# First five products begin on half of the features, and eight early transfers get a buffer each

## What is computed

```
mod = silu(c) @ w_ada + b_ada                     # 6 x 1024 columns
sh1, sc1, g1, sh2, sc2, g2 = split(mod, 6)
h   = rms_norm(x, norm1_w) * (1 + sc1) + sh1
p   = h @ w_in                                    # q, k, v, z, a, beta, ...
q, k, v = silu(causal_conv4(p[q, k, v]));  q, k = l2_normalize(q), l2_normalize(k)
g    = -exp(a_log) * softplus(p[a] + dt_bias);  beta = sigmoid(p[beta])
o    = gated_delta_rule(q, k, v, g, beta)         # 8 heads, chunks of 64
```

## Time and profile before

| | us |
|---|---|
| median of 3 runs | 970.33 (969.82 to 974.45) |
| profiled execution, its own time | 974.01 |
| its span, first to last instruction | 972.2 |
| PE busy in it | 926.5 |
| DVE busy | 667.2 |
| ACT busy | 504.9 |

### The profile page before, as it was taken

The page is one execution under the profiler, slowest core; times in us unless marked ns, Lnnn a source line. Parts: engine busy times, 40 slices in busy tenths (PEclk is TensorE's granted clock), DMA queues, the critical chain, the costliest instruction groups (busy, mean ns, idle before and its releaser), DMA issues.

```text
span 972.2 us, 18558 instructions
## 1 busy us (share of the span) xinstructions
PE 926.5 (95%) x7996; PEld 880.7 (91%) x7996; DVE 667.2 (69%) x1113; ACT 504.9 (52%) x821; POOL 65.2 (7%) x91
## 2 busy tenths in 40 slices
PE   5789999999999999999989999989999999999997
PEld 2588888898899999989989999979998999999997
DVE  3876677557579986778758875465656677777643
ACT  2476666544344556455334444465565566665442
POOL 0100012011000000030000001010000300000001
PEclk9799999999999999999999999999999999999999
DMA  8743222232249985446898775515343345555631
GB/s 321 265 157 127 88 88 91 85 131 88 88 158 359 351 299 219 174 179 253 253 290 318 265 241 186 197 43 197 131 140 108 107 177 196 186 174 166 235 120 44
DMA packets 27681, 177.31 MB, mean 182 GB/s; under 512 B 2864, under 2 KB 5680, under 8 KB 7504
## 3 DMA queue, kind: packets, MB, share of 16 engines
q1 hardware_dynamic: 27600, 176.13, 51.5%
HBM read 174.29 MB, written 1.84 MB: 181 GB/s over the span
## 4 chain that ended last, share of the span: by engine, by line
PE 71%; DVE 12%; ACT 7%; DMA 7%; issue 2%; SPq 0%; DVEq 0%; ACTq 0%
PE ps L1002 38%; PE ps L1008 19%; DVE wl L1696 3%; DMA raw<-in_w_fi_dram 3%; DVE acc L1631 2%; ACT wh L1343 2%; PE ps L1000 2%; DMA raw<-in_ada_dram 1%; DMA raw<-in_w_rest_dram 1%; DVE tmp L1658 1%; PE ps L1046 1%; DMA raw<-in_w_sc_dram 1%; PE ps L1140 1%; PE ps L1054 1%; PE ps L1201 1%
## 5 line engine op out<-in xcount | busy, mean ns | idle before, releaser
L1002 PE MATMUL ps<-HH,wh 128*128 128x256 f32 x1480 | 388.0, 294 | 6.4 <-DVE wl L1696 5.5
L1696 DVE TENSOR_TENSOR wl<-raw,wh 128x1024 fp32r<-128x1024 f32 x265 | 321.4, 1233 | 97.2 <-ACT wh L1343 96.5
L1002 PE MATMUL ps<-HH,wl 128*128 128x256 f32 x1480 | 375.2, 285 | 0.0
L1343 ACT ACTIVATE wh<-raw 128x1024 fp32r<-128x1024 f32 x265 | 272.6, 1040 | 171.8 <-PE ps L1008 105.3
L1002 PEld LDWEIGHTS ps<-HH,wh 128*128 128x128 f32 x1480 | 287.1, 194 | 15.8 <-issue 8.0
L1002 PEld LDWEIGHTS ps<-HH,wl 128*128 128x128 f32 x1480 | 287.1, 194 | 2.1 <-issue 2.1
L1008 PE MATMUL ps<-HL,wh 128*128 128x256 f32 x1480 | 241.5, 286 | 2.6 <-DVE HL L1671 2.2
L1008 PEld LDWEIGHTS ps<-HL,wh 128*128 128x128 f32 x1480 | 207.3, 194 | 3.3 <-DVE HL L1671 2.6
L1002 PE MATMUL ps<-FH,wl 128*128 128x256 f32 x352 | 88.8, 285 | 0.0
L1002 PE MATMUL ps<-FH,wh 128*128 128x256 f32 x352 | 88.1, 279 | 0.0
L1631 DVE SCALAR_TENSOR_TENSOR acc<-raw,silc,acc 128x512 f32<-128x512 f32 x101 | 76.6, 758 | 8.4 <-DMA raw<-in_ada_dram 5.2
(11 more groups left out here) (251 smaller groups left out, 1090.1 us busy)
## 6 DMA issues: line engine op xcount, KB each, us to landing
raw<-in_ada_dram SPq DMA_DIRECT2D x32, 1024.0 KB, 5.3
raw<-in_w_fi_dram SPq DMA_DIRECT2D x22, 1024.0 KB, 4.9
raw<-in_w_up_dram SPq DMA_DIRECT2D x22, 1024.0 KB, 4.8
raw<-in_w_rest_dram SPq DMA_DIRECT2D x20, 1024.0 KB, 4.8
raw<-in_w_in_dram SPq DMA_DIRECT2D x16, 1024.0 KB, 4.8
raw<-in_w_qkv_dram SPq DMA_DIRECT2D x12, 1024.0 KB, 4.8
raw<-in_w_o_dram SPq DMA_DIRECT2D x8, 1024.0 KB, 4.7
raw<-in_w_fo_dram SPq DMA_DIRECT2D x8, 1024.0 KB, 4.9
```

The lines of the kernel that those rows point to most:

```text
L1002: e.matmul(o, w[:, k, 128 * t:128 * t + 128], x_hi[:, k0 + k, :], start=first and n + k == 0, **MM)
L1343: e.activation(whl[u % HALF][0][:, 0:n], raw[i % RAW][:, c:c + n], ACT.Copy).then_inc(*a_hi.up(u))
L1696: e.tensor_tensor(wl[:, 0:n], raw[i % RAW][:, c:c + n], wh[:, 0:n].bitcast(F32), ALU.subtract).then_inc(*v_lo.up(u))
```

## The change

The first five products (q0, k0, v0, q1, k1) are cut in two. Their items are now 128 x 1024 (0.5 MB), and each product's first unit, which needs only the features 0 to 511, stands in the plan before the second half of the modulation. Their second units follow when the features 512 to 1023 are there. `ab` now stands behind these five products, and not behind q0. The eight early items of `w_ada` have a buffer each (`ada_buf`, in memory that is used by `QT`, `KT` and others later), so they wait for nothing themselves. `main` starts with five banks (0, 1, 2, 5, 6); banks 5 and 6 go to the heads' streams when the products that used them are done. Nine matmuls on constants ("warm_up") stand behind the second item of rows. The clearing of `G40` and `inv` ("zero") moves from the beginning to behind the second `parts`.

```diff
-    for b, kp in ((2, 0), (0, 0), (2, 1), (0, 1), (3, 0), (1, 0), (3, 1), (1, 1)):
-        ada_item(b, kp, rows=b == 0 or (b, kp) == (1, 0))
...
+    halved = [(open_product(kind, j, (HH, HL, N0)), a["w_in"][qkv[kind] + j])
+              for kind, j in (("q", 0), ("k", 0), ("v", 0), ("q", 1), ("k", 1))]
+    for n, (b, kp) in enumerate(((2, 0), (0, 0), (2, 1), (0, 1))):
+        ada_item(b, kp, rows=b == 0, early=n)
+    piece(*halved[0], 0, 1024)
+    for n, (b, kp) in enumerate(((3, 0), (1, 0), (3, 1), (1, 1))):
+        piece(*halved[n + 1], 0, 1024)
+        ada_item(b, kp, rows=(b, kp) == (1, 0), early=4 + n)
+    for p, w in halved:
+        piece(p, w, 1024, 1024)
+    product("ab", 0, a["wab"], (HH, HL, N0), width=128, parts=((0, 1024),))
+    for kind, j in (("v", 1), ("q", 2), ("k", 2), ("v", 2), ("q", 3), ("k", 3), ("v", 3)):
+        product(kind, j, a["w_in"][qkv[kind] + j], (HH, HL, N0))
...
-    main, misc = Ring(range(3)), Ring((3, 4))
+    main, misc = Ring((0, 1, 2, 5, 6)), Ring((3, 4))
...
-    open_streams = [(st, None) for st in range(STREAMS)]
+    open_streams = [(2, None)]
...
+    def startup():
+        emit("begin")
+        adas = [it["i"] for it in items if it["early"] is not None]
+        for i in adas[0:2]:
+            ada(i)
+        direct_norm(N0)
+        ada(adas[2])
+        drain()
+        ada(adas[3])
+        split_up_to(0)
+        low_of(0)
+        emit("warm_up")
+        drain()
+        emit("mod_scale", N0, 0)
+        for j in (0, 1):
+            scale(N0, j)
+        for j in (0, 1):
+            parts(N0, j)
+        for n, (p, _) in enumerate(halved):
+            split_up_to(n + 1)
+            low_of(n + 1)
+            open_banks(p)
+            for t in range(2):
+                emit("mm", p["units"][0], t)
+            if n < 4:
+                ada(adas[4 + n])
+            if n == 2:
+                drain()
+        drain()
+        emit("mod_scale", N0, 1)
+        for j in (2, 3):
+            scale(N0, j)
+        for j in (2, 3):
+            parts(N0, j)
+        emit("zero")
+        for p, _ in halved:
+            run_unit(p, 1)
+            close_product(p)
```

More of the change, by code:

```diff
@@ L15 @@
 RAW = 3
+EARLY_ADA = 8
 HALF = 5
@@ L221, in _program @@
     sqs = [sb(f"sq{i}", [128, 512]) for i in range(3)]
+    early = ExitStack()
+    ada_buf = [sb(f"ada{i}", [128, 2048], where=early) for i in range(EARLY_ADA)]
+    early.close()
     mixer = ExitStack()
@@ L311, in unit, with open_product, piece @@
         p["units"].append(u)
+    def open_product(kind, j, x, width=256, split=False):
+        p = dict(p=len(products), kind=kind, j=j, x=x, split=split, width=width, units=[], items=[], k=0)
+        products.append(p)
+        return p
+    def piece(p, src, at, n):
+        it = item(src[:, at:at + n], n, ada=None, rows=False)
+        p["items"].append(it["i"])
+        for c in range(0, n, 1024):
+            m = min(1024, n - c)
+            unit(it, p, c, m, m // p["width"], p["width"], p["k"])
+            p["k"] += m // p["width"]
@@ L313, in product @@
     def product(kind, j, src, x, width=256, split=False, parts=((0, 2048),)):
[L314 to L317, removed]
+        p = open_product(kind, j, x, width, split)
         for at, n in parts:
[L319 to L324, removed]
+            piece(p, src, at, n)
@@ L814, in operands_of, with run_unit, open_banks, close_product @@
         return [("parts", src, kt // 2) for kt in kts]
[L816 to L835, removed]
+    def run_unit(p, n):
+        u = p["units"][n]
+        split_up_to(u + HALF - 1)
+        low_of(u)
+        if n == 0:
+            open_banks(p)
+        until(*operands_of(p, units[u]))
+        tiles = p["width"] // 128
+        for t in range(tiles):
+            emit("mm", u, t)
+            if (n, t) != (len(p["units"]) - 1, tiles - 1):
+                tick()
+    def open_banks(p):
+        count = 2 if p["split"] else 1
+        while len(main.order) < count:
+            assert tasks
+            tick()
+        taken = [main.take() for _ in range(count)]
+        p["banks"] = [b for b, _ in taken]
+        p["free"] = [f for _, f in taken]
+    def close_product(p):
         after(p)
@@ L1158, in tensor_engine @@
                 ins.then_inc(*p_misc.up("red", blk))
+            elif kind == "warm_up":
+                for _ in range(WARM):
+                    e.matmul(psum[7][:, 0:128], ones, eye, start=True, **MM)
             elif kind == "norm_sq":
```

109 lines of the change are left out of this document (51 added, 58 removed).

## The result

The changed kernel takes 984.59 us, median of 4 runs (982.18 to 987.14), against 971.17 us for the kernel before, run beside it (4 runs, 969.82 to 974.45). The ratio is 1.012 with a 95% interval of 1.007 to 1.017: slower by some 13 us, where the interval allows 6.5 to 16.7. The profiled executions are nearer to each other: 974.01 before (span 972.2) and 982.18 after (span 980.4), 8.2 us.

A forecast was written before the change was run, and what follows sets the result against it. PE works 95% of the span, so only its waits and low-clock work count. Behind at 26 tiles 2.4, clock 3.5 and the rest 2.0 sum to 7.9 us over 970.3: 978.2 us, range 966 to 988.

The forecast's parts named there:

- Slower: Outcome class for the whole kernel: changed kernel slower than the kernel before, above 975.2 us on the median; chance 0.65.
- Start of the first product: Start of PE's products: first product matmul at 29.6 us, 10.5 us earlier than before.
- Five first halves: First-half tiles up to tile 11's end at 57.3 us: PE idle or short of operands for 4.1 us.
- v's SiLU: Ahead of v0's transposes: PE waits 6.3 us where it waited 1.99, with SiLU ending at 73.7.
- Rival A: At q0's copy on ACT: copy not held by k1's half transfer, PE waits 3.0 at v; 974.9 us, chance 0.20.
- Decays: Ahead of `G`: k1 done at 78.1, `G` at 91.2 us, PE waits 5.0 us where it waited 2.12.
- The mark of 26 tiles and the clock: At 26 product tiles: reached at 93.1 us, 2.4 behind before; low clock behind longer waits adds 3.5 (0 to 6).
- The rest: Heads, starting behind tile 26 and not 22: one more wait, 2.0 us (-2 to 5); nothing from the output projection on.
- on the median: Last step: profiled 974.0 plus 7.9 gives 981.9; carried to the median, 970.3 plus 7.9 gives 978.2 us.
- rival C: Clock and heads: low spells twice as long (+3.5) and heads at their upper bound (+3); 984.7 us, chance 0.18.

The follow-up runs named there:

- e4: Changed kernel with 30, 70 and 70 unread matmuls ahead of the second halves, v0's transposes and `G`, longer than the waits: 1003.5 us.
- e8: Changed kernel with 9, 20 and 20 unread matmuls ahead of the second halves, v0's transposes and `G`: 985.84 us.
- e9: Changed kernel with the a/b product right behind q0's second half, in bank 7: 980.52 us.
- e10: e9 with the modulation's blocks also earlier on DVE: 978.23 us.
- e12: e10 with `G` three tiles later: 978.96 us.
- e1: Changed kernel with no product halved and a/b behind q0, keeping the eight buffers, warm-up matmuls and five banks: 984.41 us.
- e11: As e5, but ACT copies the second row ahead of the weight splits, and four dummies stand at another place: 973.24 us.
- e7: Kernel before with only the a/b product moved, from behind q0 to behind k1: 986.73 us.
- e3: Changed kernel with v0's transposes four tiles later and `G` two tiles later: 984.77 us.
- e6: Changed kernel with the modulation's blocks earlier on DVE, same order of products: 986.95 us.
- e5: As e1, but the modulation's blocks stand on DVE in order of landing, ahead of the first scaling: 975.26 us.

## Why the prediction was right, and where it was not

Slower was forecast at 0.65, and the time lay in the range. The mechanism, a lead lost at v0's SiLU and at `G` to chains over ACT and DVE, is in the rows. That the profiled executions differ by 8.2 us where 7.9 was forecast is in part luck: at the mark they stand 9.8 apart, and 1.6 of it went behind the mark, where this execution of before had low spells that the one of after had not. The medians stand 13.4 us apart, 5.5 more than forecast. Step by step:

*Start of the first product:* 29.80, forecast 29.6. Within it one term was off: nine warm-up matmuls took 2.27 us and not 1.5, since I had priced them by transposes. The start of the transposes was 0.3 earlier, and their bank did hold them.

*Five first halves:* ten half tiles ended at 51.9 (forecast 51.1), DVE made `w1c` at 53.19 (52.8), tile 11 ended at 58.19 (57.3). DVE's wait for the turn is there, 3.60.

*v's SiLU:* PE went on at 74.63 (forecast 73.7) after 5.01 us (6.3), since the low clock let it arrive later. The chain is the one forecast, row by row, 1.0 later since the half landed at 62.7 and not at 61.7: its split at 62.72, copy at 63.68, three convolutions without a gap. Rival A fell with it: the copy was held.

*Decays:* wait 5.05 (forecast 5.0), `G` at 93.64 (91.2). ACT's walk from the copy of k1 to `kdc` took the 9.9 forecast (80.59 to 90.48). What was late was k1, 80.6 for 78.1: 0.9 came with v, 1.6 by the low clock behind v0 (e4).

*The mark of 26 tiles and the clock:* 97.42, where 93.1 + 3.5 = 96.6 was forecast. The clock's cost up to here is 3.2: the 1.6 behind v0, and 1.6 behind `G`, where the step to the first head took 3.7 us and in e8, with the clock up, 2.15. I had forecast 3.5, about half at each place, so this term held, and v's 0.9 makes up the rest. That low time ahead of v0's wait costs nothing held too (e8). But the spell behind `G` goes on for 5 us behind the 26 tiles, where I had taken spells of 3.4 us.

*The rest:* forecast +2.0. With 26 tiles at 97.42 the change was 97.42 - 90.7 = 6.7 behind; at the `gb` mark 9.8, at the end 8.2. So the heads cost 3.1 and not 2.0, inside the bounds of -2 to 5. Some 1.5 of it goes with the low clock (in e8 the lead over the changed kernel grows from 1.9 at the first head to 3.4 at the mark). The waits are 2.6 more (with the clock 4.1, not 3.1: the 90.7 holds an estimate of 2.9). Three that the kernel before doesn't have, 7.1 us, stand in the heads' last steps (from 50 to 310 us):

```profile
PE ps L1138 <- DVE lc L1623: 3.4, 2, 2.3
...
PE ps L1141 <- DVE v L1627: 2.0, 2, 1.4
PE ps L1132 <- DVE v L1620: 1.7, 1, 1.7
```

Against them, 3.5 us less is waited in the heads' other steps (1.8 for 5.3) and 1.0 less at the later transposes of v. These three waits are the same in e9, e10 and e12, so they don't come from a/b's place; e1 and e11, with five banks and no halves, don't have them. They go with the halves or with the order that the halves bring.

*The step that was mis-sized* is the last: "on the median". I carried the 7.9 of one execution over to the medians. But 974.01 was 2.8 above the median of before, and 982.18 was 2.4 below that of after; 8.2 + 2.8 + 2.4 = 13.4. How large the miss is, four runs of each don't settle, since the interval of 6.5 to 16.7 us holds 7.9 too; in the later series before's median was up to 972.8, which would leave some 12. That the median, 984.6, falls on rival C's 984.7 is chance: C asked for 7.0 us by low spells and 5.0 in the heads besides, and up to the mark the rows have 4.7 and 1.6. The late start of before's profiled execution (40.08, and 38.40 in e7) can be a part of the 2.8. Another part is seen: the four runs of after are two near 980.5 (span, mean clock 0.984 and 0.982) and two near 985.1 (0.977), so what separates them is time at the low clock, and the profile is one of the first two. Why the kernel before falls to it less often in its median run than in its profiled one, and whether the changed order makes such spells likelier, is open.

*What the explanation missed.* I gave the lead's loss to two longer waits. e3, e6 and e12 show that these waits are not places that can be repaired one at a time. Filled in e3 and e12, they came back at the next chain (6.97 at v1, 6.72 at v0); an earlier second half in e6 only made the wait at v0 longer (6.98). ACT ended all three. And I priced a/b's late place at some 5 us (3 in `G`'s wait, 2.0 in the heads). Alone it costs 14.0 (e7). In the changed kernel, putting it back is worth 4.1 (e9), and the eager modulation 2.3 more (e10). The parts don't add: each decides which chain meets which on ACT. What is left in e10, 5.4 us, goes with the halves, as e11 without them is even with before; in its rows stand the wait of 6.92 for `G`, and ACT held by a half transfer. How much each is worth was not measured. That the second of these is due to a ring of three buffers that holds only half as many bytes was not tried.

## What to carry to other kernels

A lead on PE was worth nothing here, where other engines ended the next wait; count their work up to the place where they catch up, and expect a filled wait to reappear at the next one. A small product that heads a long chain is to be moved by itself first: here the move of a/b, which looks like a detail beside eight buffers and ten halves, costs as much alone as the whole change. And a buffer of its own brings a transfer forward only if nothing that waits stands ahead of it in the queue that issues it.

## What was not expected of the hardware

A matmul of `ones` with `eye`, 128 columns in full FP32, took 0.226 us at the full clock (70 in 15.8 us, each shown as two records), while one of the products' matmuls on fp32r parts, with twice the columns, takes 0.12 (8 in 0.96).

The low clock followed waits of only 2.0 to 2.2 us in both kernels (and 0.52 from 55.0 to 61.4 behind the wait of 2.21), but not each such wait: in e5 it stayed at 1.00 behind 1.94 and 1.99. Unread matmuls in the waits kept it at 1.00 where they filled them but for 0.6 us or less at a time (9 and 20 in e8, 70 in e4); where 20 of them left a wait of 2.34 us it fell to 0.67. What decides between waits of equal length these runs don't show.
